# A two-layer decoder step on one core: down slabs of the next experts issued from ScalarE's DMA queue, gate and up slabs from the sync engine's as before

## The reference, cut to what matters

```python
def moe_swiglu(x, wr, br, w1, w3, w2):
    logits = (x @ wr).astype(jnp.float32) + br.astype(jnp.float32)
    top_val, top_idx = lax.top_k(logits, TOP_K)
    gates = jax.nn.softmax(top_val, axis=-1)
    combine = jnp.einsum('btk,btke->bte', gates, jax.nn.one_hot(top_idx, N_EXPERTS, dtype=jnp.float32))
    y = jnp.zeros_like(x)
    for e in range(N_EXPERTS):
        h = jax.nn.silu(x @ w1[e]) * (x @ w3[e])
        y = y + (combine[..., e:e + 1].astype(x.dtype) * h) @ w2[e]
    return y
```

## Time and profile before

| | us |
|---|---|
| median of three executions | 874.85 (872.93 to 876.83) |
| the profiled execution, its own time | 873.78 |
| span of the profiled execution, first to last instruction | 872.1 |
| TensorE busy in the span | 829.2 |
| VectorE, ScalarE, GpSimd busy | 246.7, 139.6, 99.0 |
| moved by DMA | 206.41 MB |

### The profile page before, as it was taken

One profiled execution on the slowest core, in us unless ns is written; L12 is line 12 of the kernel. 1 busy time (PEld: TensorE's weight loads), 2 busy tenths in 40 slices (PEclk: granted clock), 3 DMA queues, 4 the chain that ended last, 5 costly groups with the idle time before them and its releaser, 6 DMA issues.

```text
span 872.1 us, 13706 instructions
## 1 busy us (share of the span) xinstructions
PE 829.2 (95%) x5824; PEld 558.7 (64%) x5824; DVE 246.7 (28%) x706; ACT 139.6 (16%) x342; POOL 99.0 (11%) x146
## 2 busy tenths in 40 slices
PE   6999999999999999999987979999998899999996
PEld 5888878888888888868675666862443244443432
DVE  2173215000000000074577751255222010121025
ACT  0020113000000111131216661121000010000010
POOL 4300300000000000031212310004100001101120
PEclk9999999999999999999998989987999999999998
DMA  9899723538240048895023471956999999999971
GB/s 297 281 373 353 253 94 96 182 108 259 67 132 1 26 141 264 189 232 152 26 97 106 163 313 59 408 210 250 385 404 401 402 399 407 393 394 410 396 292 50
DMA packets 106587, 206.41 MB, mean 237 GB/s; under 512 B 23558, under 2 KB 60818, under 8 KB 105508
## 3 DMA queue, kind: packets, MB, share of 16 engines
q1 hardware_dynamic: 93540, 166.68, 54.2%
q0 software_dynamic: 9360, 32.34, 10.5%
q10 hardware_dynamic: 3632, 6.59, 2.2%
HBM read 192.90 MB, written 12.69 MB: 236 GB/s over the span
## 4 chain that ended last, share of the span: by engine, by line
PE 86%; DVE 6%; DMA 3%; ACT 2%; issue 2%; SPq 1%; DVEq 0%; ACTq 0%
PE ps L673 45%; PE ps L1236 16%; PE ps L1264 7%; DMA slot<-moe_w 2%; PE ps L724 2%; PE ps L1303 2%; PE ps L1060 1%; PE ps L1003 1%; PE ps L1203 1%; PE ps L1011 1%; PE ps L1076 1%; PE ps L1029 1%; PE ps L886 1%; PE ps L1043 1%; PE ps L1253 1%
## 5 line engine op out<-in xcount | busy, mean ns | idle before, releaser
L1236 PE MATMUL ps<-slot,hT 128*32 128x512 f32 x1408 | 157.4, 606 | 6.0 <-DMA slot<-moe_w 4.7
L673 PE MATMUL ps<-rw,slot 128*128 128x264 f32 x640 | 142.6, 385 | 0.0
L673 PEld LDWEIGHTS ps<-rw,slot 128*128 128x128 f32 x640 | 120.8, 189 | 21.6
L673 PE MATMUL ps<-xw,slot 128*128 128x264 f32 x512 | 118.5, 387 | 0.8 <-issue 0.8
L1236 PEld LDWEIGHTS ps<-slot,hT 128*32 128x32 f32 x1408 | 46.7, 112 | 112.1 <-issue 105.4
L673 PEld LDWEIGHTS ps<-xw,slot 128*128 128x128 f32 x512 | 95.5, 189 | 18.8 <-issue 2.3
L673 PE MATMUL ps<-hT,slot 128*128 128x264 f32 x352 | 79.8, 386 | 0.0
L673 PEld LDWEIGHTS ps<-hT,slot 128*128 128x128 f32 x352 | 66.3, 190 | 10.9
L1264 PE MATMUL ps<-slot,hT 128*32 128x256 f32 x1216 | 68.3, 380 | 0.7 <-DMA slot<-moe_w 0.7
L673 PE MATMUL ps<-yT,slot 128*128 128x264 f32 x256 | 59.4, 388 | 0.5 <-ACT yT L1528 0.5
L1264 PEld LDWEIGHTS ps<-slot,hT 128*32 128x32 f32 x1216 | 38.2, 110 | 26.8 <-DMA slot<-moe_w 1.2
(11 more groups left out here) (465 smaller groups left out, 829.9 us busy)
## 6 DMA issues: line engine op xcount, KB each, us to landing
slot<-moe_w SPq DMA_DIRECT2D x64, 1024.0 KB, 18.6
slot<-moe_w SPq DMA_DIRECT2D x16, 2048.0 KB
slot<-ffn_w SPq DMA_DIRECT2D x22, 1024.0 KB, 11.0
slot<-ffn_w SPq DMA_DIRECT2D x8, 1408.0 KB, 6.5
slot<-w_in_even SPq DMA_DIRECT2D x4, 2048.0 KB, 13.2
r_rows<-silu ACTq DMA_DIRECT2D x1, 6144.0 KB, 32.0
slot<-w_out_even SPq DMA_DIRECT2D x2, 2048.0 KB, 24.0
slot<-w_in_odd SPq DMA_DIRECT2D x2, 2048.0 KB, 9.2
```

What stands on the lines that cost most here:

```text
L673: mm = pe.matmul(out, lhs(k), rhs(k), start=(k == 0), stop=(k == n - 1))
L1236: mm = pe.matmul(ps[t][32 * j:32 * j + 32, :].rearrange("p (w n) -> p w n", w=2), xgT[:, cap * k + 32 * t:cap * k + 32 * t + 32], moe_slab ...
```

## The change

SP keeps the loads of slots 0 to 3 and loses those of slots 4 and 5 for experts 1 and up; expert 0 is loaded as before. ScalarE gets them: at the end of its part of pass i it reads the expert number (`next_down(i + 1)`), waits for `m_used`, issues slot 4, waits for `w2_done`, issues slot 5, and goes on with the silus of the next pass. Destinations, sources, sizes and semaphores of the loads are the same.

```diff
@@ next_expert of the sync engine
                 sp.wait_ge(w13_done, tiles_at(i))
                 load_expert(3, e)
-                sp.wait_ge(m_used, i)
-                load_expert(4, e)
-                sp.wait_ge(w2_done, tiles_at(i))
-                load_expert(5, e)
@@ scalar engine
+            act.wait_ge(list_ready, 1)
+
+            def next_down(i):
+                e = act.value_load(qlist[0:1, i:i + 1] if isinstance(i, int) else qlist[0:1, bass.ds(i, 1)],
+                                   min_val=0, max_val=2 * NE - 1) % NE
+                act.wait_ge(m_used, i)
+                for s in (4, 5):
+                    if s == 5:
+                        act.wait_ge(w2_done, tiles_at(i))
+                    rows = moe_w2[0][bass.ds(e, 1), CH * (s - 4):CH * (s - 4) + CH, :]
+                    act.dma_start(moe_slab(s), rows.rearrange("e (k p) n -> p (e k) n", p=P)).then_inc(slab_in[s], 16)
+
             def one_pass(i, nt):
@@
                 for t in range(nt):
                     act.wait_ge(h_t, base + t + 1)
                     act.copy(hTs[:, t].rearrange("p h q -> p (h q)"), ps[turned[t]][:, 0:256]).then_inc(h_copied, 1)
+                next_down(i + 1)
```

## The result

The changed kernel took 887.06 us (median of six executions, 883.31 to 889.72) beside 875.84 for the kernel before on the same chips: ratio 1.0135, 95% interval 1.0115 to 1.0155, so 11.8 us or 1.35% slower (the two medians by themselves lie 11.2 us apart). Run a second time beside the last experiments it came to 1.0166 (1.0141 to 1.0191), 14.5 us. The forecast was 884.3, slower, with a range of 877 to 889. In its terms, beside the median of 874.85, the first timing is 886.7 and the second 889.4, just past the top of the range. The profiled execution took 889.54 us with a span of 887.8, 15.7 us more than the span of before; it lies 2.5 us above its median and the profile of before 2 us under its own, so the trace shows more than the medians do.

What follows compares the result with a forecast made beforehand. DMA was taken to be full in the experts' passes, with weights landing barely ahead of TensorE's use. Pass 2's 6.1 and pass 5's 3.3, with zero elsewhere, made +9.4 us: 884.3 us, range 877 to 889.

Steps and rivals of the forecast that it cites:

- What bounds the passes: Experts' passes: DMA is full, three-tile passes also fill TensorE, and weights land barely ahead of use.
- Equal shares packet by packet: SP's and ACT's backlogged queues alternate packets; with 4 KB rows on both, about 204 GB/s each.
- Pass 2: Expert 2: slot 3 usable at 674.2 instead of 663.97, 10.2 us late; less credited waits, net +6.1 us.
- Passes 3 and 4: Slot 3 of expert 3 arrives by 707, needed at 708; pass 4 keeps the four-tile lead: +0.
- Pass 5: Expert 5: slot 3 lands at 775.3, needed at 772.05, so TensorE loses +3.3 us.
- The total of the waits: TensorE waits 14.7 us for slabs instead of 5.4: 11.4 in pass 2, 3.3 in pass 5.
- DMA, always busy, delivers that byte when it does now: Passes 6 and 7: the expert's last byte comes no later than before, so the cost does not recur.
- the recurring rival: Passes 5 to 7: late TensorE frees slots late, DMA runs dry, each pays 3.3: sum 16, 891 us; 10%.
- Passes 6 and 7: Slack grown to 10.0 and 9.5 us against a delay of at most 10.3: +0 to +0.8.
- ACT: ScalarE's two issues cost 0.8 us, covered because the next silus wait for TensorE anyway: cost 0.
- The sum: Whole kernel: 6.1 + 0 + 3.3 + 0 = +9.4 us, bounds 6.9 and 10.2.

Runs made afterwards that it cites:

- e9: The change, but ScalarE issues slot 4 only after slot 2 landed, SP the next expert's slot 0 only after slot 4 landed; ratio 1.0000 to the kernel before.
- e10: All slabs of experts 1 and up on ScalarE's queue in order of use, none on the sync engine's; ratio 1.0142 to the kernel before, +12.4 us.
- e11: The change again, unaltered, timed beside the last experiments; ratio 1.0166 to the kernel before, +14.5 us.
- e6: The change with each down slab loaded as four quarters of its columns, 1 KB packets; ratio 1.0439 to the kernel before, +38.4 us.
- e1: Only expert 2's down slabs on ScalarE's queue, those of all other experts on the sync engine's; ratio 1.0032 to the kernel before, +2.8 us.
- e7: The change with 9 idle matmuls before the wait for slot 2 of pass 2 and 11 before slot 3; ratio 1.0136 to the kernel before, +11.9 us.
- e8: The change with 12 idle matmuls before TensorE's wait for slot 3 of pass 5; ratio 1.0123 to the kernel before, +10.8 us.
- b1: The kernel before with 7 idle matmuls before TensorE's wait for slot 0 of pass 3; ratio 1.0008 to the kernel before, +0.7 us.

## Why the prediction was right

The direction and the mechanism were right, and the time lay in the range. The size was low, 9.4 us against 11.8 and, the second time, 14.5, and part of what fits does so by luck, as said below.

- *What bounds the passes, and that the order of landing is what the change alters.* Shown by e9, which gives all of the time back by two waits that restore the order.
- *Equal shares packet by packet.* Right, and shown more sharply than by the earlier trace rows: 1030 to 981 packets with 2 KB rows, 1203 to 1212 with 1 KB. In the change itself, with 4 KB rows on both, it is 634 to 530 over 652 to 664.
- *Pass 2.* Slot 3 usable at 674.36, predicted 674.2. The start of pass 3 came 7.45 us late instead of 6.1: the term left out that slot 3's matmuls run at half clock behind the stall, 5.09 us instead of 3.5. The fall behind slot 2 cost nothing, slot 3 wasn't there yet. It only made the wait before slot 3 shorter, so that the two waits of pass 2 are 9.6 us where 11.4 were predicted.
- *Passes 3 and 4.* +0 was predicted and -1.9 came: the clock fall at the start of pass 3 of before, behind its wait of 3.41, is gone. The two things left out, +1.35 and -1.9, nearly cancel: that pass 4 starts 5.55 late, close to the 6.1 predicted, is luck.
- *Pass 5.* Needed at 777.03 - 5.01 = 772.02 (predicted 772.05), landed at 777.0 (predicted 775.3): +5.3 with the 0.31 before slot 2, instead of +3.3. The total of the waits, 15.0 against 14.7 predicted, fits only because pass 2 has 1.8 too little and pass 5 some 2 too much. What went wrong in pass 5 is "DMA, always busy, delivers that byte when it does now". The four-tile pass 3, itself late, frees slots 4 and 5 late, and SP has nothing to load at that moment: of q1's packets only 17 fall in 728 to 732 and none in 732 to 737, and slot 5 is issued at 733.4. The stretch 724 to 737 of the changed kernel:

```profile
724.00:737.00 13.00, 13.00 (x212) 6.70 (x208) 1.70 (x4) 0.00 (x0) 2.19 (x4) 1.00 0.91 303
```

  and the one of before in which TensorE stands at about the same place, 717 to 730:

```profile
717.00:730.00 13.00, 13.00 (x218) 7.05 (x220) 1.70 (x4) 0.37 (x1) 1.56 (x3) 1.00 1.02 384
```

  81 GB/s less over 13 us are 1.05 MB or 2.6 us of DMA, once; the slab came 1.7 us after its forecast. That the one made the other is read from the trace, no run tests it. This is the mechanism of the recurring rival, in one place and not in every pass. On top came the clock, 8.32 us for what takes 5.15: +3.2.
- *Passes 6 and 7.* +0, as predicted.
- *ACT.* Its 14 issues took 0.38 us each, and its silus still wait for TensorE. Right for the change. In e10, with all slabs on ACT's queue, it no longer holds.
- *The sum.* 5.55 + 5.3 + 3.2 + 0, and 1.7 for a clock fall in the last pass, make 15.75 of the 15.7 us of span. The prediction's sum of 9.4 had no term for the clock, which in this execution is worth 1.7 + 1.7 + 3.4 + 1.7 against 1.7 before, 6.8 us, the part behind slot 2 of pass 2 hidden. The last fall, at 854, stands behind idle times that both kernels have, and the trace of e11, the same kernel with the same idle times, has none there (its last 32 down matmuls take 13.97 us), so it belongs to this execution and not to the change. The ratio of the first timing, 2.4 us above the forecast, has less of all this than the trace.

What stays open: how much of the spread between the two timings of the change (1.0135 and 1.0166) is the clock. The profiled execution of the repeat, 884.43 us, waits 7.23 us before slot 2 of pass 2 and 1.10 before slot 3 instead of 4.34 and 5.29, and has a granted clock of 0.94 over 640 to 700 and 0.96 over 760 to 800, 3.6 + 1.6 = 5.2 us of work lost against 8.5 above, which fits its shorter time; but its median was the higher one, so one trace each does not settle it.

## What to carry to other kernels

When DMA is full and weights land just ahead of use, a queue is also a schedule. Moving some loads to a second engine's queue lets later-needed slabs run beside, and so ahead of, earlier-needed ones, and the price is the bytes that are put in front of the next wait, until the consumer has fallen behind by as much; if loads must be split, make each queue wait for the landing on the other, as e9 does. Don't give a queue that fills up to an engine whose arithmetic is on the path. And look at the clock behind each new stall of several microseconds: the matmuls there took up to 1.6 times as long in the trace, and it costs only where nothing behind them waits for DMA anyway. That filling the stalls gives time back was not shown here.

## What the runs showed of the hardware

Two hardware queues with work waiting shared the DMA engines by packets, so the row size set the shares: 4 KB rows took 2.0 times the bytes of 2 KB rows and 3.8 times those of 1 KB rows (3.97 to 1.96 and 4.60 to 1.21 MB in 15 us). With both queues full the total stayed at 402 and 395 GB/s, against 408 for one queue with 4 KB rows. An issue behind several waiting slabs holds its engine: up to 10.10 us of ScalarE in e6, 13.28 us for five loads in e10, 0.38 us each in the change, where at most two slabs were in the queue. After stalls of TensorE of 3.4 to 5.3 us (before and after the change), and after one of 2.4 in e9, the granted clock was at its lower level for 3.4 to 6.9 us; in e1 it was not after a stall of 3.16 us that came a few microseconds behind another fall. Stalls of pass 2 (e7), pass 5 (e8) and pass 3 (b1) filled with idle matmuls left it at 1.00.
